# A two-layer hybrid trunk on one core: the norm's inverse root moved behind the input projections, the norm weight put on x ahead of them

## The chip, the cores and the metric

One core of a Trainium2 chip runs the whole kernel. The metric is device time in microseconds (us) of one launch. The kernel before takes 2810.47 us (median of 3 runs, 2808.8 to 2810.52).

## The reference, cut to what matters

256 tokens of width 4096 go through two layers. Each layer starts with an RMS norm and one wide input projection (w_in), whose columns feed four branches (S5, latent attention "MLA", gated linear attention "GLA", RG-LRU). The four results are gated and go through one output projection (w_out), which is added to x. A last RMS norm ends the trunk.

```python
def rms_norm(x, g):
    y = x * rsqrt(mean(x * x, axis=-1) + 1e-6)   # one inverse root r per token
    return y * g                                 # one weight g per column of x
# per layer:
h = rms_norm(x, norm_g)
z = h @ w_in      # = r * ((x * g) @ w_in): r belongs to the token, g to the summed index
# ... four branches on the columns of z, concatenated to y ...
x = x + y @ w_out
# at the end: out = rms_norm(x, final_g)
```

The latents of MLA (cq, ckv) are RMS-normalised again before they are used, and the gate columns of z go through SiLU.

## The kernel before

**Tiling.** Activations lie transposed: 128 partitions are 128 columns of x, 256 tokens lie along the free axis, and x is 32 such tiles (`zb`). Every large product is computed to float32 accuracy from two halves. An operand v is split into hi = v rounded to float32r and lo = v - hi. A chunk is 2 tiles of the summed index by 256 output columns, 256 KB of weights. For a chunk TensorE runs 4 matmuls of 512 columns (hi with hi and lo together) and 4 of 256 columns (lo with hi), lines 322, 323 and 325 in `chunk`. A layer has 914 chunks. 32 of them make a pair: two halves of 16 chunks, one for each half of the four accumulator banks.

**Stages of a layer.** Nine pairs of input projection, in which the S5 work of DVE and GpSimd goes on beside them ("pre" pairs); a middle stage (GLA values, S5's GLU, heads of MLA); eight gate pairs, one for each 128 columns of the branches; and eight pairs of output projection. The hb tiles hold the split activations.

**Order.** Every engine has its own instruction stream, written out by hand, in which a step number c (the chunk) says where small work goes. At step c ScalarE (ACT) copies the hi half of the weights of chunk c+3 (`hi`, line 626), once chunk c-1 is done, because `w2` has 4 buffers; VectorE (DVE) subtracts to get the lo half (`lo`, line 1049); TensorE runs chunk c. So DVE may be some three chunks late before TensorE stands. The sync engine (SP) loads weights into 8 raw buffers, each as soon as its old content is used. Finished accumulators are taken out by ACT (`evac`, line 632) and added by DVE (line 1055).

**The norm before.** In the prologue, ACT squares x as its eight parts of 512 KB land (line 649), DVE sums them (line 1181), GpSimd adds the sums (line 1638). TensorE turns the sums into one column per 128 tokens (`columns`, line 333, 12 matmuls), ACT takes the square root (line 637), DVE the reciprocal (line 1060), TensorE spreads it over the partitions (`spread`, line 342). Only then does DVE multiply x by g and r in one operation per tile (`h_mul`, line 1068), ACT rounds it (`split_hi`, line 642) and GpSimd subtracts (`split_lo`, line 1648); chunks 0 to 15 of a layer each wait for their pair of tiles. The same sequence stands between the two layers, behind the last evacuation. At the end, DVE multiplies the 32 tiles by r and final_g (line 1618), and four stores of 1 MB write them. The angles of the rotary embedding are also computed in the prologue (lines 1166 to 1173).

Of the kernel before, what the change touches and what calls it, by code (L numbers as in the profile page):

```python
# [18 lines left out]
P = 128  # L19
L = 2  # L20
# [50 lines left out]
PART_AT = {c + n: (p, kind, i, n, chunks) for p, (kind, i, c, chunks) in enumerate(PARTS) for n in range(chunks)}  # L71
Y_LAST = {5: 0, 8: 1, 11: 2, 16: 3, 21: 4, 22: 5}
# [22 lines left out]
def trunk(nc, w, x, pos, const, small, pg_in, s5raw, mixw_d, s5w_d, wg2_d, out):  # L95
# [3 lines left out]
    with ctx:  # L99
# [67 lines left out]
        rcol = sb("rcol", [P, 12])  # L167
        s5_all = sb("s5_all", [P, L, 3, 32])
# [26 lines left out]
        squares_made, sx_ready, x_ready = sem("squares_made"), sem("sx_ready"), sem("x_ready")  # L195
# [29 lines left out]
        x_added, x_saved = sem("x_added"), sem("x_saved")  # L225
# [39 lines left out]
        def _(sp):  # L265
            sp.dma_start(posi[:, :], pos.partition_broadcast(P)).then_inc(pos_loaded, 16)
            sp.dma_start(sm_all[:, :, :], small).then_inc(sm_loaded, 16)
            for i in range(8):
                sp.dma_start(zb[:, 4 * i:4 * i + 4, :], x[:, 4 * i:4 * i + 4, :]).then_inc(x_loaded[i], 16)
            sp.dma_start(kc[:, :], const).then_inc(const_loaded, 16)  # L270
            for s in range(RAW):
                sp.dma_start(raw[:, s], w[s]).then_inc(raw_loaded[s], 16)
# [26 lines left out]
            sp.wait_ge(x_stored, 16 * (1 + 16 * L))  # L299
# [3 lines left out]
        def _(pe):  # L303
# [83 lines left out]
            pe.wait_ge(const_loaded, 16)  # L387
            pe.wait_ge(consts_made, 1)

            for l in range(L):  # L390
                n_l, h_l, c_l = l * N_LAYER, l * H_LAYER, l * C_LAYER

                pe.wait_ge(sx_ready, l + 1)
                pe.wait_ge(last_squared, l + 1)
                columns([(sx, ssq[:, 0, :], ssq[:, 1, :])], B_Y)
                spread([ps[:, B_BU, 0:T]], c_l + 1)

                for c in range(CH_PAIR):
                    if c % CH_HALF == 0:
                        pe.wait_ge(acc_read, h_l + c // CH_HALF + 1)  # L400
# [19 lines left out]
                def k_turn():  # L420
                    pe.wait_ge(acc_read, h_l + H_MID + 2)
# [187 lines left out]
            pe.wait_ge(sx_ready, L + 1)  # L609
            pe.wait_ge(last_squared, L + 1)  # L610
# [5 lines left out]
        def _(act):  # L616
# [4 lines left out]
            def hi(n0, c, count=1):  # L621
# [4 lines left out]
                A(w2[:, d, :, 0, :], raw[:, s, :, :], ACT.Copy).then_inc(hi_ready, count)  # L626

# [17 lines left out]
            for i in range(8):  # L645
                act.wait_ge(x_loaded[i], 16)
                if i >= 2:
                    act.wait_ge(x_ready, i - 1)
                A(sqx[:, 4 * (i % 2):4 * (i % 2) + 4, :], zb[:, 4 * i:4 * i + 4, :], ACT.Square).then_inc(squares_made, 1)
                if i == 1:  # L650

                    act.wait_ge(consts_made, 1)
                    act.wait_ge(rope_made, 1)
                    A(gb[0:64, :], ga[0:64, :], ACT.Abs).then_inc(act_prep, 1)
                    act.wait_ge(act_prep, 1)
                    A(rope[0:64, :], gb[0:64, :], ACT.Sin, bias=HALF_PI[0:64], scale=-1.0).then_inc(act_prep, 1)
                    A(rope[64:96, :], ga[64:96, :], ACT.Sin, scale=-1.0).then_inc(act_prep, 1)
                    A(rope[96:128, :], ga[96:128, :], ACT.Sin).then_inc(act_prep, 1)

            for s in range(LOOK):  # L660
                act.wait_ge(raw_loaded[s], 16)
                act.wait_ge(chunk_done, s + 1)
                A(w2[:, s, :, 0, :], raw[:, s, :, :], ACT.Copy).then_inc(hi_ready, 1)

# [17 lines left out]
            def s5_inputs(it, g):  # L682

                act.wait_ge(bu_ready, it + 1)
                A(us[:, :], zb[:, g + Z_S5, :], ACT.Copy).then_inc(us_ready, 1)
# [7 lines left out]
            def s5_steps(it, g, more=True):  # L693
# [3 lines left out]
                if more:  # L697
                    steps[25] = [lambda: s5_inputs(it + 1, g + 1)]
# [3 lines left out]
            for l in range(L):  # L702
                n_l, h_l, c_l = l * N_LAYER, l * H_LAYER, l * C_LAYER
                rms(c_l + 1, 2, D, EPS1)
                split_hi(0, l * 32 + 1)
                split_hi(1, l * 32 + 2)
# [26 lines left out]
                pre_pair(1, {0: [lam_exponent], 2: [turn_sines], 25: [lambda: s5_inputs(l * G8, 0)],  # L733
                             31: [lambda: s5_tables(l * G8, 0)]}, one=True)
                own.restart()
                pre_pair(2, s5_steps(l * G8, 0))
                own.restart()
                with act.Fori(3, 8) as i:
                    pre_pair(i, s5_steps(l * G8 + (i - 2), i - 2))
                    own.restart()  # L740
                pre_pair(8, s5_steps(l * G8 + 6, 6))
# [8 lines left out]
                def latent_root():  # L750
                    act.wait_ge(cols_ready, c_l + 2)
                    A(ncol[:, 0:2], ps[:, B_Y, 0:2], ACT.Sqrt, bias=EPS1, scale=1.0 / QR)
                    A(ncol[:, 2:4], ps[:, B_Y, 2:4], ACT.Sqrt, bias=EPS1, scale=1.0 / KVR).then_inc(rms_ready, 1)
# [57 lines left out]
                for c in range(MID_END):  # L811
# [7 lines left out]
                    if c % CH_HALF == CH_HALF - 1 and (c < MID_GLU or MID_V3 <= c < MID_QKV):  # L819
                        h = H_MID + (c // CH_HALF if c < MID_GLU else 7)  # L820
                        evac(h_l + h, h % 2, n_l + (N_MID + c + 1))
                own.restart()

                for u in (9, 10, 14):
# [10 lines left out]
                def gate_pair(g, last=False):  # L835
# [102 lines left out]
                    def first_silu():  # L938
                        act.wait_ge(acc_read, h0 + 3)
# [5 lines left out]
                    def second_silu():  # L945
                        act.wait_ge(acc_read, h0 + 4)
# [17 lines left out]
                    for c in range(CH_PAIR):  # L964
                        if c > 0:
# [11 lines left out]
                hi(n_l + N_GATE, 0)  # L977
# [11 lines left out]
                def out_store(i, h, more):  # L989

                    act.wait_ge(outx, l * 16 + (i * 2 + (h + 1)))
                    act.dma_start(xres[:, bass.ds(i * 4 + 2 * h, 2), :], zb[:, bass.ds(i * 4 + 2 * h, 2), :]).then_inc(x_stored, 16)
                    if more:
                        old_x(h, bass.ds(i * 4 + (4 + 2 * h), 2))

                for c in range(CH_PAIR):
# [946 lines left out]
```

## Time and profile before

| | before |
|---|---|
| median of 3 runs | 2810.47 us |
| the profiled execution's own time | 2810.84 us |
| its span, first to last instruction | 2809.1 us |
| TensorE (PE) matmul busy | 2743.7 us, 98% of the span |
| VectorE (DVE) | 2065.9 us, 74% |
| ScalarE (ACT) | 1593.1 us, 57% |
| GpSimd (POOL) | 782.0 us, 28% |
| mean granted TensorE clock | 0.994 |

Busy time is the time in which an engine has an instruction under way. What is left of the span beside TensorE's 2743.7 us is some 65 us, and the stretches of the profile say where it lies. "Idle before" names the engine and line that ended a wait.

### The profile page before, as it was taken

How to read it: one execution, taken by the hardware profiler on the slowest of the kernel's cores; microseconds unless marked ns; L12 is line 12 of the kernel's file. 1: busy time of each engine (PE TensorE's matmuls, PEld its weight loads, DVE VectorE, ACT ScalarE, POOL GpSimd, SP SyncE). 2: the span in 40 equal slices, each digit the busy share in tenths (PEclk: the TensorE clock that was granted, in tenths of full speed). 3: DMA queues.
4: the chain of work that ended last, by engine and by line, in shares of the span. 5: the costliest groups of instructions: out<-in, count | busy, mean ns of one | idle time of the engine just before them, and what ended most of it. 6: DMA issues, size and time to landing. Idle time of an engine off the chain costs nothing.

```text
span 2809.1 us, 54381 instructions
## 1 busy us (share of the span) xinstructions
PE 2743.7 (98%) x15960; PEld 2358.4 (84%) x15960; DVE 2065.9 (74%) x3372; ACT 1593.1 (57%) x2867; POOL 782.0 (28%) x823
## 2 busy tenths in 40 slices
PE   5999999999999999999999999999999999999997
PEld 4888888888888888888878888888888888888886
DVE  8899999766666676555588999997666666855555
ACT  5555555656656665444455555556666656644443
POOL 3255555400110132111134555552011111411111
PEclk9999999999999999999999999999999999999998
DMA  6765566585655547777647666666765565577765
GB/s 218 254 189 173 185 177 188 168 262 175 187 174 168 188 148 219 210 210 210 207 143 210 179 183 175 187 176 184 248 188 170 172 185 166 178 213 210 210 210 175
DMA packets 294180, 538.72 MB, mean 192 GB/s; under 512 B 32432, under 2 KB 43584, under 8 KB 293056
## 3 DMA queue, kind: packets, MB, share of 16 engines
q1 hardware_dynamic: 268736, 497.45, 58.9%
q10 hardware_dynamic: 25344, 39.99, 4.2%
q8 instruction: 56, 0.92, 0.1%
q14 instruction: 44, 0.36, 0.0%
HBM read 516.34 MB, written 25.17 MB: 193 GB/s over the span
## 4 chain that ended last, share of the span: by engine, by line
PE 86%; DVE 7%; issue 3%; ACT 2%; POOL 1%; DMA 0%; ACTq 0%; DVEq 0%; SPq 0%; POOLq 0%
PE ps L323 53%; PE ps L322 26%; DVE w L1049 3%; PE ps L325 1%; ACT w L626 1%; DVE yy L1118 1%; POOL lg L1672 1%; DVE g L1112 1%; PE ps L354 1%; PE ps L333 1%; PE ps L365 0%; DVE zb L1618 0%; PE ps L342 0%; PE ps L502 0%; PE ps L501 0%
## 5 line engine op out<-in xcount | busy, mean ns | idle before, releaser
L323 PE MATMUL ps<-hb,w 128*128 128x512 f32 x5824 | 2051.9, 396 | 6.1 <-issue 6.1
L1049 DVE TENSOR_TENSOR w<-raw,w 128x512 fp32r<-128x512 f32 x1828 | 1338.0, 741 | 643.0 <-ACT w L626 633.0
L626 ACT ACTIVATE w<-raw 128x512 fp32r<-128x512 f32 x1828 | 1133.3, 628 | 935.6 <-PE ps L323 917.0
L322 PE MATMUL ps<-hb,w 128*128 128x256 f32 x5690 | 1617.1, 284 | 8.3 <-DVE w L1049 6.8
L323 PEld LDWEIGHTS ps<-hb,w 128*128 128x128 f32 x5824 | 1091.3, 188 | 254.5 <-issue 6.6
L322 PEld LDWEIGHTS ps<-hb,w 128*128 128x128 f32 x5690 | 1074.9, 189 | 44.5 <-DVE w L1049 17.4
L323 PE MATMUL ps<-gl,w 128*128 128x512 f32 x800 | 283.3, 395 | 0.0
L1810 POOL TENSOR_TENSOR nf<-zb 128x256 f32 (+1 forms) x60 | 52.0, 867 | 537.1 <-DVE zb L1586 531.6
L322 PE MATMUL ps<-gl,w 128*128 128x256 f32 x680 | 190.2, 280 | 0.0
L323 PE MATMUL ps<-w,hb 128*128 128x512 f32 x512 | 180.6, 395 | 0.0
L323 PEld LDWEIGHTS ps<-gl,w 128*128 128x128 f32 x800 | 149.5, 188 | 30.1
L1652 POOL TENSOR_TENSOR sx<-yl 128x256 f32<-128x256 f32 x16 | 15.7, 984 | 473.5 <-DVE yl L1452 473.5
L322 PE MATMUL ps<-w,hb 128*128 128x256 f32 x496 | 141.6, 286 | 1.5 <-DVE w L1049 1.0
L322 PEld LDWEIGHTS ps<-gl,w 128*128 128x128 f32 x680 | 128.1, 188 | 2.5
L1661 POOL TENSOR_SCALAR sx<-kc,pgp 128x256 f32<-128x256 f32 x64 | 73.3, 1145 | 185.2 <-POOLq L252 107.4
L323 PEld LDWEIGHTS ps<-w,hb 128*128 128x128 f32 x512 | 95.8, 188 | 21.2
L632 ACT ACTIVATE half_lo<-ps 128x512 f32<-128x512 f32 (+1 forms) x144 | 84.2, 585 | 42.3 <-PE ps L323 42.3
L1118 DVE TENSOR_TENSOR yy<-g,tab 128x512 f32<-128x512 f32 x64 | 103.9, 1623 | 0.0
L322 PEld LDWEIGHTS ps<-w,hb 128*128 128x128 f32 x496 | 93.6, 189 | 7.3 <-DVE w L1049 6.2
L1112 DVE TENSOR_TENSOR_SCAN g<-pgd,yy 128x256 f32<-128x256 f32 x128 | 86.8, 717 | 0.0
L1663 POOL TENSOR_SCALAR nf<-nf 128x256 f32<-128x256 f32 x64 | 64.2, 1003 | 5.6
L1652 POOL TENSOR_TENSOR sx<-yg 128x256 f32<-128x256 f32 x16 | 10.6, 662 | 187.8 <-ACT yg L920 187.8
(311 smaller groups left out, 2410.0 us busy)
## 6 DMA issues: line engine op xcount, KB each, us to landing
raw<-in_w SPq DMA_DIRECT2D x1843, 256.0 KB, 2.8
hd<-heads ACTq DMA_DIRECT2D x16, 512.0 KB, 5.2
gate<-xres ACTq DMA_DIRECT2D x32, 256.0 KB, 4.3
xres<-zb ACTq DMA_DIRECT2D x32, 256.0 KB, 3.6
zb<-in_x SPq DMA_DIRECT2D x8, 512.0 KB, 7.3
xres<-in_x SPq DMA_DIRECT2D x4, 1024.0 KB, 6.4
s5w<-in_s5w ACTq DMA_DIRECT2D x16, 256.0 KB, 3.4
out<-zb SPq DMA_DIRECT2D x4, 1024.0 KB, 3.9
```

The lines of the kernel that those rows point to most:

```text
L322: mm(acc[:, T:], a_lo, m_hi, start=False, stop=False, skip_group_check=True)
L323: last = mm(acc, a_hi, m_both, start=(k == 0), stop=(k == nk - 1), skip_group_check=True)
L325: last = mm(acc[:, T:], a_lo, m_hi, start=False, stop=False, skip_group_check=True)
L333: last = mm(ps[:, bank, 2 * i + b:2 * i + b + 1], s[:, P * b:P * b + P], ones[:, :], start=(n == 0), stop=(n == len(tiles) - 1))
L626: A(w2[:, d, :, 0, :], raw[:, s, :, :], ACT.Copy).then_inc(hi_ready, count)
L632: A(half_lo[:, 0:tiles, :], ps[:, 2 * half:2 * half + tiles, 0:T], ACT.Copy).then_inc(lo_copied, 1)
L1049: V.tensor_tensor(w2[:, d, :, 1, :], raw[:, s, :, :], w2[:, d, :, 0, :].bitcast(F), ALU.subtract).then_inc(w2_ready, count)
L1112: V.tensor_tensor_scan(g2[:, a, :], pgd[:, j:j + 1].to_broadcast([P, T]), yy[:, a, :], 0.0, ALU.mult, ALU.add).then_inc(scanned, 1)
L1118: V.tensor_tensor(yy[:, :, :], g2[:, ::-1, :], tab[:, 1:3, :], ALU.mult).then_inc(tab_used, 1)
L1661: own.do(G.tensor_scalar(sx[:, :], iota, f0, None, ALU.mult))
L1663: own.chain(G.tensor_scalar(nf[:, :], nf[:, :], -MAGIC, None, ALU.add))
L1810: own.chain(G.tensor_tensor(nf[:, :], z, z, ALU.mult))
```

## The change

Layer 0: x is multiplied by g alone as it arrives (DVE, one operation of two tiles), split by ACT and GpSimd, and the chunks start. The squares are summed by TensorE between chunks (`x_sums`, eight times 8 matmuls of one column). Root, reciprocal and spread come in steps 17 to 21 of the first pair; the rotary angles move to steps 19 and 23. Layer 1: ACT multiplies each new pair of x tiles by the next g during the output stage (`x_gain`), in the last output pair ACT and GpSimd split 15 of the 16 pairs of tiles, and the first pair of layer 1 only handles the last one; root in steps 6 to 10. The inverse root is kept as a spread tile `rs` and as a column `rch`, and is multiplied to results: `scale` (13 a layer) and `gates_scale` (16 a layer) are new DVE operations of 128x512 (one of the 13 is 128x256); the GLA values take it inside their evacuation (4 a layer, ACT and DVE each in two operations of 128x256); MLA's latents take it inside their own root. At the end ACT has put final_g on 30 tiles before, and DVE multiplies two tiles at a time by r. Two of the weight loads are issued behind each of the first four parts of x. In the gate stage a second chunk's hi and lo come ahead of the waits at each pair's border.

```diff
@@ SP
             for i in range(8):
                 sp.dma_start(zb[:, 4 * i:4 * i + 4, :], x[:, 4 * i:4 * i + 4, :]).then_inc(x_loaded[i], 16)
+                for s in range(2 * i, min(2 * i + 2, RAW)):
+                    sp.dma_start(raw[:, s], w[s]).then_inc(raw_loaded[s], 16)
             sp.dma_start(kc[:, :], const).then_inc(const_loaded, 16)
-            for s in range(RAW):
-                sp.dma_start(raw[:, s], w[s]).then_inc(raw_loaded[s], 16)
@@ PE
+            def x_sums(i):
+                pe.wait_ge(squares_made, i + 1)
+                pe.wait_ge(consts_made, 1)
+                for b in range(2):
+                    for q in range(4):
+                        last = mm(ps[:, (B_Y, B_A)[b], 0:1], sqx[:, 4 * (i % 2) + q, P * b:P * b + P], ones[:, :], ...)
+                last.then_inc(squares_used if i < 7 else cols_ready, 1)
-                pe.wait_ge(sx_ready, l + 1)
-                pe.wait_ge(last_squared, l + 1)
-                columns([(sx, ssq[:, 0, :], ssq[:, 1, :])], B_Y)
-                spread([ps[:, B_BU, 0:T]], c_l + 1)
                 for c in range(CH_PAIR):
...
                     chunk(n_l, c, c // CH_HALF)
+                    if l == 0 and c in X_SUMS:              # 2, 4, ... 16
+                        x_sums(X_SUMS.index(c))
+                    if l > 0 and c == ROOT_AT[l] - 1:       # ROOT_AT = (17, 6)
+                        pe.wait_ge(sx_ready, l)
+                        pe.wait_ge(last_squared, l)
+                        columns([(sx, ssq[:, 0, :], ssq[:, 1, :])], B_Y)
+                    if c == ROOT_AT[l] + 2:
+                        pe.wait_ge(const_loaded, 16)
+                        spread([ps[:, B_BU, 0:T]], c_l + 1)
@@ ACT
                 for c in range(CH_PAIR):
                     hi(n_l, c)
-                    if c + 2 < CH_HALF:
-                        split_hi(c + 2, l * 32 + (c + 3))
+                    if l == 0 and c + 2 < CH_HALF:
+                        split_hi(c + 2, c + 3)
+                    if l == 0 and c in (1, 3, 5, 7, 9, 11, 13):
+                        x_square((c + 1) // 2)
+                    if l == 0 and c == 23:
+                        rope_sines()
+                    if l > 0 and c == 0:
+                        last_x(l - 1)                       # waits for the last sum, squares it, stores it
+                    if l > 0 and c == 2:
+                        split_hi(15, l * 32 + 16)
+                    if c == ROOT_AT[l]: ...                 # the root
@@ ACT, middle to gate stage
+                hi(n_l + N_GATE, 0)
+                hi(n_l + N_GATE, 1)
                 for u in (9, 10, 14):
                     act.wait_ge(part_stored[u % 3], ...)
...
                 nc.scalar.preload_act_table_set("silu_and_others")
-                hi(n_l + N_GATE, 0)
+                act.wait_ge(scaled, l * 13 + 13)
@@ ACT, gate pair (DVE's has the same order)
                     def second_silu():
-                        act.wait_ge(acc_read, h0 + 4)
+                        act.wait_ge(gates_scaled, l * 16 + (g * 2 + 2))
...
                     if not last:
                         second_gates()
                         hi(n0, CH_PAIR)
+                        hi(n0, CH_PAIR + 1)
                         second_silu()
@@ ACT, output stage
+                def x_gain(i, h):
+                    act.wait_ge(x_squared, l * 15 + (i * 2 + (h + 1)))
+                    if l < L - 1:
+                        act.wait_ge(x_stored, 16 * (16 * l + 1) + (i * 32 + 16 * (h + 1)))
+                    for q in range(2):                      # z = one tile of x, gain = its column of g
+                        last = A(z, z, ACT.Identity, scale=gain)
+                    last.then_inc(x_gained, 1)
+                def split_x(p):                             # steps 4, 7, 10, 13, 21 to 31 of the last pair
+                    ...
+                    A(hb[:, 2 * p:2 * p + 2, 0, :], zb[:, 2 * p:2 * p + 2, :], ACT.Copy).then_inc(h_hi_ready, 1)
@@ DVE
+            def h_mul(p, l):
+                ...
+                V.tensor_tensor(hf[p % 3][:, :, :], zb[:, 2 * p:2 * p + 2, :], g, ALU.mult)
+            def scale(z, half):
+                dve.wait_ge(acc_read, half + 3)
+                V.tensor_tensor(z, z, spread_rs(z.shape[1]), ALU.mult).then_inc(scaled, 1)
...
                 for c in range(CH_PAIR):
                     lo(n_l, c)
-                    if c + 3 < CH_HALF:
-                        h_mul(c + 3, l * 32)
+                    if l == 0 and c + 3 < CH_HALF:
+                        h_mul(c + 3, l)
+                    if l > 0 and c == 1:
+                        h_mul(15, l)
+                    if c == ROOT_AT[l] + 1:
+                        layer_root()
+                    if c == ROOT_AT[l] + 4:
+                        layer_rs()
+                    if l == 0 and c == 19:
+                        rope_angles()
+                    if c == 22:
+                        scale(zb[:, 0:2, :], h_l)
+                    # unchanged: preparation of S5 at steps 16, 18, 20, ... 30
...
+                    def gates_scale(h):
+                        dve.wait_ge(acc_read, h0 + (h + 3))
+                        V.tensor_tensor(gate[:, h, :, :], gate[:, h, :, :], spread_rs(2), ALU.mult)
@@ DVE, the end
-            for k in range(KT):
-                last = V.scalar_tensor_tensor(out=zb[:, k, :], ..., in1=ps[:, B_BU, 0:T], ...)
+            for k in range(0, KT - 2, 2):
+                last = V.tensor_tensor(zb[:, k:k + 2, :], zb[:, k:k + 2, :],
+                                       ps[:, B_BU:B_BU + 1, 0:T].to_broadcast([P, 2, T]), ALU.mult)
@@ POOL
-            for i in range(1, 6):
-                G.tensor_tensor(sx[:, :], sx[:, :], ...)    # sums of the squares of x
+                def x_lo(p):                                # pairs 0 to 3, then 4 to 14, in the last output pair
+                    pool.wait_ge(h_hi_ready, (l + 1) * 32 + (p + 1))
+                    G.tensor_tensor(hb[:, 2 * p:2 * p + 2, 1, :], zb[:, 2 * p:2 * p + 2, :], ..., ALU.subtract)
```

## Rows read from the trace of the kernel before

**Rows 1.** Stretches of the span: for each engine busy us (instructions), then granted clock, DMA.

```profile
0.00:59.70 59.70, 31.58 (x145) 24.94 (x146) 47.94 (x69) 34.30 (x51) 25.82 (x31) 1.00 0.65 212
59.70:1402.30 1342.60, 1337.78 (x7829) 1152.22 (x7827) 987.76 (x1608) 768.52 (x1389) 365.65 (x388) 1.00 0.64 195
1402.30:1441.30 39.00, 32.05 (x145) 25.40 (x146) 29.75 (x53) 20.16 (x35) 21.53 (x16) 0.82 0.37 114
1441.30:2784.80 1343.50, 1338.37 (x7829) 1152.30 (x7827) 986.29 (x1608) 768.66 (x1390) 368.99 (x388) 1.00 0.63 190
2784.80:2809.10 24.30, 3.91 (x16) 3.56 (x16) 14.20 (x36) 1.48 (x3) 0.00 (x0) 0.55 0.45 184
```

**Rows 2.** Chain of waits, first 60 us: start, us, what.

```profile
24.05 2.70 PE ps L333 x12
...
41.51 0.78 DVE yy L1068 x2
42.30 0.92 DVE w L1049
```

**Rows 3.** Timeline of the first 62 us: start, us, instruction, [idle before].

```profile
6.23 1.06 ACT L649 ACTIVATE vb<-zb 128x1024 f32<-128x1024 f32 x1 [4.20 <-DMA zb<-in_x]
...
30.25 1.27 POOL L1648 TENSOR_TENSOR hb<-xx,hb 128x512 fp32r<-128x512 f32 x1 [9.27 <-ACT hb L642]
```

**Rows 4.** TensorE's timeline, first chunks of the two halves of pair 0.

```profile
59.80 0.28 PE L325 MATMUL ps<-hb,w 128*128 128x256 f32 x1
...
81.99 0.28 PE L325 MATMUL ps<-hb,w 128*128 128x256 f32 x1
```

**Rows 5.** Chain of waits between the layers.

```profile
1402.32 0.61 ACT half_lo L632
...
1409.70 3.03 issue
```

**Rows 6.** TensorE's timeline, middle stage: columns between two chunks.

```profile
522.39 0.95 PE L333 MATMUL ps<-ones,ssq 128*128 128x1 f32 x8
523.20 0.36 PE L322 MATMUL ps<-w,hb 128*128 128x256 f32 x1
```

**Rows 7.** VectorE's timeline: rotary angles to the first sum; second half of pair 0.

```profile
4.34 0.29 DVE L1166 CAST gab<-kext 128x256 f32<-128x256 int32 x1 [4.34 <-DMA sm_all<-in_small]
...
7.42 1.96 DVE L1181 TENSOR_REDUCE sx<-vb 128x256 f32<-128x1024 f32 x1
...
66.37 1.29 DVE L1049 TENSOR_TENSOR w<-raw,w 128x512 fp32r<-128x512 f32 x2
...
82.59 0.69 DVE L1055 TENSOR_TENSOR zb<-half_lo,ps 128x512 f32<-128x512 f32 x1 [0.25 <-ACT half_lo L632]
```

**Rows 8.** VectorE's timeline, middle stage, GpSimd busy beside it.

```profile
502.84 3.99 DVE L1049 TENSOR_TENSOR w<-raw,w 128x512 fp32r<-128x512 f32 x4
```

**Rows 9.** Timelines of ScalarE and VectorE at the border of two gate pairs.

```profile
779.82 0.60 ACT L632 ACTIVATE half_lo<-ps 128x512 f32<-128x512 f32 x1 [0.78 <-PE ps L323]
...
783.68 1.47 DVE L1049 TENSOR_TENSOR w<-raw,w 128x512 fp32r<-128x512 f32 x2 [0.84 <-ACT w L626]
...
785.98 0.69 DVE L1049 TENSOR_TENSOR w<-raw,w 128x512 fp32r<-128x512 f32 x1
```

**Rows 10.** Timeline from the middle to the gate stage.

```profile
626.81 1.28 ACT L976 ACT_TABLE_LOAD   x1 [1.42 <-ACTq L252]
...
629.51 0.38 PE L322 MATMUL ps<-hb,w 128*128 128x256 f32 x1 [1.05 <-DVE w L1049]
```

**Rows 11.** Timeline of the end; then the page's part on DMA issues.

```profile
2792.15 12.62 DVE L1618 SCALAR_TENSOR_TENSOR zb<-zb,sm,ps 128x256 f32<-128x256 f32 x32 [1.31 <-PE ps L342]
2795.40 9.74 SPq L296 DMA_DIRECT2D out<-zb  x4
...
zb<-in_x SPq DMA_DIRECT2D x8, 512.0 KB, 7.3
...
out<-zb SPq DMA_DIRECT2D x4, 1024.0 KB, 3.9
```

More of the change, by code:

```diff
@@ L626, in hi, with tokens_evac @@
                 A(w2[:, d, :, 0, :], raw[:, s, :, :], ACT.Copy).then_inc(hi_ready, count)
+            def tokens_evac(h0, half, n_done):
+                act.wait_ge(chunk_done, n_done + W2)
+                act.wait_ge(acc_read, h0 + 2)
+                for j in range(2):
+                    last = A(half_lo[:, j, :], ps[:, 2 * half + j, 0:T], ACT.Identity, scale=rch[:, j:j + 1])
+                last.then_inc(lo_copied, 1)
             def evac(h0, half, n_done, tiles=2):
@@ L697, in s5_steps @@
                 if more:
-                    steps[25] = [lambda: s5_inputs(it + 1, g + 1)]
+                    steps[25] = [lambda: s5_inputs(it + 1, g + 1, ready)]
                     steps[31] = [lambda: s5_tables(it + 1, 0)]
@@ L751, in latent_root @@
                     act.wait_ge(cols_ready, c_l + 2)
-                    A(ncol[:, 0:2], ps[:, B_Y, 0:2], ACT.Sqrt, bias=EPS1, scale=1.0 / QR)
-                    A(ncol[:, 2:4], ps[:, B_Y, 2:4], ACT.Sqrt, bias=EPS1, scale=1.0 / KVR).then_inc(rms_ready, 1)
+                    for i in range(4):
+                        last = A(ncol[:, i:i + 1], ps[:, B_Y, i:i + 1], ACT.Sqrt, bias=EPS1, scale=rvar[:, i:i + 1])
+                    last.then_inc(rms_ready, 1)
                 def glu_evac(m):
@@ L1139, in s5_skip, with s5_steps @@
                 own.do(V.tensor_copy(pgd[:, 4:5], pgl[:, g, C_S5D:C_S5D + 1]))
-            def s5_steps(it, g, first=False, more=True):
+            def s5_steps(it, g, ready=None, first=False, more=True):
                 steps = {}
@@ L1147, in s5_steps @@
                 steps[3] = [lambda: s5_scalars(g)] + steps[3]
-                steps[6] = ([] if first else [lambda: s5_tail(it - 1, g - 1)]) + [lambda: s5_skip(g)]
+                steps[6] = ([] if first else [lambda: s5_tail(it - 1, g - 1, ready)]) + [lambda: s5_skip(g)]
                 return steps
@@ L1331, in _, with pre_pair @@
                         evac(h_l + h, h, zb[:, 2 * h:2 * h + 2, :])
+                scale(zb[:, 2:4, :], h_l + 1)
                 own.restart()
[L1334 removed]
+                def pre_pair(i, steps, dst=None, scales=()):
                     for c in range(CH_PAIR):
@@ L1407, in _ @@
                 steps[73] = steps.get(73, []) + [lambda: reciprocals(c_l + 3, 2)]
+                for n in range(8):
+                    at = MID_QKV + 5 * n + 1
+                    z = zb[:, Z_QK + 2 * n:Z_QK + 2 * n + 2, :]
+                    steps[at] = steps.get(at, []) + [lambda n=n, z=z: scale(z, h_l + (6 + n))]
                 for c in range(MID_END):
@@ L1610, in _ @@
                             out_end(i, 0)
+                with dve.Fori(1, 8) as i:
+                    out_pair(i)
                 out_end(7, 1)
@@ L1714, in _ @@
                 h_l, c_l = l * H_LAYER, l * C_LAYER
-                for k in range(KT // 2):
+                for k in range(KT // 2) if l == 0 else (15,):
                     split_lo(k, l * 32 + (k + 1))
+                pool.wait_ge(const_loaded, 16)
                 pool.wait_ge(dve_prep, l + 1)
@@ L1816, in _ @@
                     own.restart()
+                if l < L - 1:
+                    for p in range(4):
+                        x_lo(p)
                 out_squares(7, 0)
@@ L1819, in _ @@
                 pool.sem_inc(sx_ready, 1)
+                if l < L - 1:
+                    for p in range(4, 15):
+                        x_lo(p)
 def _constants():
```

233 lines of the change are left out of this document (145 added, 88 removed).

## The prediction

> **What bounds the kernel now.** I read the stretches first, then the chain of waits, then the timelines. The stretches [rows 1] show two kinds of time. In 59.7 to 1402.3 and in 1441.3 to 2784.8 us TensorE (PE) has a matmul under way for 1337.8 of 1342.6 and 1338.4 of 1343.5 us: it is the bound, and it stands for 10 us in all. The other three stretches are different: the first 59.7 us hold 145 PE instructions, the 39.0 us between the layers hold 145, the last 24.3 us hold 16. Sixteen chunks at full pace would need little: pair 0's chunk 16 starts at 59.80 and chunk 32 at 81.99 [rows 4], so a chunk is 22.19 / 16 = 1.39 us and sixteen are 22.2. In the first stretch PE waits 24 us for the sum of squares, then goes at the pace of DVE, which needs 0.78 us for h_mul and 0.92 for lo, 1.70 per chunk [rows 2]. Between the layers the same chain runs again from 1402.32 until a last gap of 3.03 us before the first chunk [rows 5], and the clock is granted at 0.82 on the mean there [rows 1], the low level of 1.2 GHz after PE had stood. So there are three places to win, and all else must stay under a PE that is always busy.
>
> **Start, layer 0.** The first part of x can be read at 6.23 us [rows 3]; then come DVE's multiply (0.7), ACT's split (0.60, by the 128x512 of [rows 9]) and GpSimd's subtraction (1.27 [rows 3]), which with handovers is 9.1 us for chunk 0. Pace after that, for each chunk. PE: 1.39 plus half of a group of 8 columns; such a group pushed the next chunk back by 523.20 - 522.39 = 0.81 [rows 6], so 1.80. ACT: two copies of 0.60 and half a square of 1.06 [rows 3, 9], 1.73. DVE: two operations that read SBUF alone; one takes 0.60 undisturbed (two in 1.29, the first of them 0.60 [rows 7]) and 3.99 / 4 = 1.00 beside a busy GpSimd [rows 8]. In GpSimd's 1.27 DVE does 0.76 of its 1.20, the rest takes 0.44, so 1.71. Three engines within 0.1 us of each other do not run at the best of them: I take 1.85, 29.6 for sixteen. I add 2.4 for the filling (the first chunks pass through the three engines one behind the other, and PE starts at the low clock) and 1.4 for data: eight parts of x, each landing 7.3 us after its issue [rows 11], now share the engines with weights, and chunk 8 is loaded last of all. Chunk 16 starts at 9.1 + 29.6 + 2.4 + 1.4 = 42.5 in place of 59.80: **-17.3**. Ends: 1.80 a chunk with nothing added gives -21.9; 2.47 (below) gives -7.4.
>
> **Second half of pair 0, layer 0.** DVE has no idle time from before 66.37 until 0.25 us ahead of 82.59 [rows 7]; it is late already, under the cover of the three chunks that are prepared ahead. The change adds at steps 18 to 22: five small operations of the root (1.0), the rotary angles (4.34 to 7.42, 3.08 [rows 7]), the copy of rs (0.35) and a scale (0.60), 5.0 in all. The cover: step 19's lo ends at 66.97 and its chunk 22 starts at 59.80 + 6 x 1.39 = 68.1, 1.2 us; later steps have about 1.7. PE is itself put back by the last group of columns and the spread, 0.81 + 0.5. So PE stands 5.0 - 1.7 - 1.3 = 2.0, and 0.4 for the scale behind step 31: **+3.7** with the 1.3. If the cover were gone, +5.4 + 1.3; if DVE caught up, +1.3. ACT's two table loads there (1.28 each, [rows 10]) lie in that cover.
>
> **Between the layers.** Chunk 16 of layer 1 starts 39.0 us after layer 0's last chunk; with 15 pairs of tiles ready it is sixteen chunks, 22.2, plus what PE now does among them: 12 columns at 0.10 and a spread of 4 matmuls, 0.5. 39.0 - 22.2 - 1.7 gives **-15.1**. What covers the rest: in the last output pair ACT has two copies a chunk, 1.2 of 1.39 us, and GpSimd 1.27 of 1.39; both keep up, barely. x_gain waits for the store of its tiles, nine steps after its issue. `last_x` holds ACT at step 0 until DVE's second sum, about 2.1 us after the last chunk; behind it in ACT's queue are a square, a DMA issue and step 1's hi, and PE has three chunks, 4.2 us. Root operations at step 7 meet a DVE with half its time free. Ends: -5 (ACT late by a chunk or two, and PE at the low clock again) and -16.8.
>
> **Middle to gate stage.** PE stood 1.05 us for DVE, which stood for ACT, which waited 1.42 for stored parts and loaded a table (1.28) before its hi [rows 10]. Two hi's now go ahead: **-2.0** for two layers. Next late is step 2's hi, with two chunks of room.
>
> **Operations added under a busy PE.** 29 of DVE a layer. Most cost nothing while PE is the bound. Where DVE is the late one they count: 0.35 for kg before S5's first step, and 0.6 to 0.75 where the last gate pair meets the output stage (DVE multiplies y there each step), 0.15 for the values: 1.25 a layer, **+2.5**. Below nothing is excluded, since they only add.
>
> **Borders of gate pairs, 14 of them.** Queued behind the added wait on ACT (silu for gates_scale) is step 2's hi; PE waits for that. The last chunk ends at 779.8 [rows 9]. Before, DVE prepared chunks 4 and 5 in one go from 783.68, a full loop restart (0.84) after the gating. Now chunk 4 is ready by 783.0, ahead of the wait; then gates_scale, silu, gating and restart put chunk 5's lo at 784.95 to 785.55, and PE needs it at 779.8 + 5 x 1.39 = 786.75. 1.2 us are left, as before: 0. GpSimd's copies wait for the gating too, and land within that.
>
> **End.** 32 operations take 12.62, 0.394 each [rows 11]. Fifteen of two tiles with r in PSUM at 0.60 (as DVE's sum of [rows 7], start to start) and two old ones are 9.8, so 2.8 less. The last store begins behind the last of them and takes 3.9 [rows 11]; the four could now queue behind one another, so **-2.5**. Ends 0 and -2.8.
>
> Sum: -17.3 + 3.7 - 15.1 - 2.0 + 2.5 - 2.5 = -30.7. From the profiled execution's 2810.84 that is 2780.1; the median of the runs, 2810.47, is 0.4 below it, inside the rounding. **2780 us.**
>
> **Rivals.**
> 1. *DVE and GpSimd shut each other out at the start.* Then a chunk costs 2 x 0.60 + 1.27 = 2.47, sixteen 39.5, and the time is 2790. For it: DVE's 1.00 in place of 0.60 [rows 8]. Against it: before, lo beside GpSimd's subtraction would then need 0.60 + 1.27 = 1.87 a chunk, and the chunk took 1.70 [rows 2]. Chance 0.12. The Trainium skill (SBUF — State Buffer, on the shared port pair) states this as a rule: a DVE operation with both inputs in SBUF and a GpSimd operation that reads SBUF hold the pair in turn for the whole instruction, so h_mul, which leaves PSUM, would pay; by that rule the time is this rival's, and the trace bears the slowing out but not the full exclusion.
> 2. *The gate pairs' borders stall.* If the 1.2 us are gone and one more is missing, 14 borders cost 14 us: 2794. For it: ACT now waits twice for DVE in a pair. Against: PE stands nowhere in the gate pairs now, and 4.8 us in the whole stretch [rows 1]. 0.07.
> 3. *The last output pair's splits come late.* ACT has 1.2 of 1.39 us; with evacuations it falls behind, PE stands and falls to the low clock: 10 us less won, 2790. 0.05.
> 4. *More is won.* The start runs at 1.80 with no data wait and DVE's lag is absorbed: 4 + 2 us more, 2774. 0.12.
> 5. *Slower than before.* The price is each of the 58 added DVE operations on PE's path, because DVE is the late engine in S5 and gate stages: at 1.00 each (beside GpSimd [rows 8]) 58 us, less the 2.5 counted: 2836; at 0.60, 2812, no change. It decides from (30.7 + 2.5 + 5.6) / 58 = 0.67 us each. For it: DVE's 988 us in the long stretch are in part dense. Against: the S5 pairs proper get none of them, and DVE is at 74% there on the mean [rows 1]. 0.04, half of it slower.
>
> **How the numbers follow.** Forecast 0.60 (2774 to 2786 on its own); the rivals as given. From 2810.47, 0.2% (5.6 us, about what a measurement can tell from none) is 2804.9 and 2816.1. All but rival 5 are faster: 0.95 with rounding; same 0.02; slower 0.03. The range reaches to rivals 1, 3 and 4 and as far as rival 2: 2771 to 2794.
>
> **What would show it.** Chunk 0 at 9 us and chunk 16 at 42 to 43; a chunk every 1.85 us before; PE gaps of some 2 us in all between 45 and 70 us, with DVE busy throughout; no gap over 1 us and a clock of 1.00 between the layers, chunk 16 of layer 1 some 24 us after layer 0's last; no wait of 1.05 at the gate stage; DVE's last stretch 9.8. I would be wrong if PE gaps repeat at each gate pair, if GpSimd's subtractions and DVE's multiplies alternate strictly at the start, or if the start waits for weights by more than 2 us.

## The result: 2795.1 us, 0.55% less than before, and the profile after

The median of five runs is 2795.13 us (2791.7 to 2797.0) against 2810.47 before; the ratio is 0.9945, with a 95% interval of 0.993 to 0.996. The kernel is faster, but the forecast of 2780 is 15 us too low and the range ended 1.1 us short. The profiled execution took 2791.7 us (span 2789.9), 3.4 us less than the median, so 11.6 us of the miss can be read in the trace.

The stretches of the changed kernel, cut where [rows 1] were cut (columns as there):

```profile
0.00:48.60 48.60, 38.17 (x241) 34.02 (x242) 31.62 (x36) 28.29 (x44) 23.50 (x26) 1.00 0.78 273
48.60:1399.40 1350.80, 1341.84 (x7850) 1155.11 (x7849) 1018.82 (x1655) 793.60 (x1449) 387.39 (x401) 1.00 0.63 193
1399.40:1425.20 25.80, 24.77 (x146) 21.32 (x145) 17.65 (x28) 11.31 (x21) 5.33 (x4) 1.00 0.57 185
1425.20:2765.00 1339.80, 1334.99 (x7810) 1149.99 (x7809) 1008.02 (x1640) 779.65 (x1423) 365.93 (x388) 1.00 0.62 188
2765.00:2789.90 24.90, 6.47 (x36) 5.42 (x34) 13.45 (x23) 2.75 (x5) 0.00 (x0) 0.64 0.41 169
```

The first stretch went from 59.7 to 48.6 us and TensorE has work in 38.2 of them. Between the layers the granted clock is 1.00 (before 0.82). TensorE's first matmul is at 9.7 us. Its timeline, at the matmul by which chunks 0, 16 and 32 can be told (it answers to [rows 4]):

```profile
10.27 0.41 PE L332 MATMUL ps<-hb,w 128*128 128x256 f32 x1
...
48.63 0.28 PE L332 MATMUL ps<-hb,w 128*128 128x256 f32 x1
...
76.49 0.28 PE L332 MATMUL ps<-hb,w 128*128 128x256 f32 x1
```

Chunk 16 came 11.2 us earlier and not 17.3, and the half behind it took 27.9 us and not 25.9. The starts of all 144 halves in both traces (the "marks" below) divide the change of the span as follows (us, after minus before):

| Step | Forecast | Traces |
|---|---|---|
| start, to chunk 16 | -17.3 | -11.2 |
| second half of pair 0, layer 0 | +3.7 | +5.7 |
| between the layers | -15.1 | -13.4 |
| middle to gate stage, two layers | -2.0 | -2.2 |
| added VectorE operations elsewhere | +2.5 | +4.7 |
| borders of gate pairs | 0 | 0 |
| end | -2.5 | -2.8 |
| sum | -30.7 | -19.2 |

The row between the layers runs to chunk 32 of layer 1. To chunk 16, where the forecast for it ended, the traces give -13.0; the half behind it took 22.19 us for 22.60, a difference that halves of one kernel also show among themselves.

How the start runs now. TensorE's timeline at the third group of column sums, to be held against [rows 6]:

```profile
26.73 1.84 PE L401 MATMUL ps<-ones,vb 128*128 128x1 f32 x16
28.43 0.36 PE L329 MATMUL ps<-hb,w 128*128 128x256 f32 x1
```

The group puts the next chunk back by 28.43 - 26.73 = 1.70 us, twice the 0.81 that I took from [rows 6]. The cause is in the counts: a matmul of these float32 sums stands as two instructions in the trace, so the "x8" of [rows 6] were four matmuls, and the "x16" here are the eight of the code. (The chunks' matmuls, which take float32r, stand as one each. The 12 and 4 that I counted for the columns and the spread were instructions too, of six and two matmuls; their price, taken per instruction, was not hurt by it.) TensorE's period is thus some 2 x 1.46 + 1.70 = 4.62 us for two chunks (most groups start 4.59 to 4.61 apart), and behind its first matmul no single gap of over 0.3 us shows up to 48 us. In the same stretch the timeline of VectorE (DVE) and GpSimd (POOL) shows something else:

```profile
19.24 1.30 POOL L1788 TENSOR_TENSOR hb<-yy,hb 128x512 fp32r<-128x512 f32 x1 [0.39 <-ACT hb L669]
19.32 1.77 DVE L1150 TENSOR_TENSOR g<-zb,sm_all 128x512 f32<-128x512 f32 x1
...
21.62 0.68 DVE L1150 TENSOR_TENSOR xx<-zb,sm_all 128x512 f32<-128x512 f32 x1
21.84 1.59 POOL L1788 TENSOR_TENSOR hb<-g,hb 128x512 fp32r<-128x512 f32 x1 [1.29 <-ACT hb L669]
```

The multiply by the norm weight takes 0.68 us alone, and 1.77 when GpSimd's subtraction has begun 0.08 before it: it ends 0.55 behind the subtraction. The other way round the subtraction takes 1.59. This is the strict alternation that the prediction named as a sign against itself. So there were two explanations of the lost 6.1 us, TensorE's matmuls or the exclusion, and the experiments had to tell them apart.

### The profile page after: what moved, and what is told of

It is laid out like the page before. It is cut to its first block, busy times and chain, and to the rows that moved or that the text cites. A ratio compares the mean times of both kernels' runs of the same rounds, so it can differ in the third digit from the quotient of the medians.

```text
span 2789.9 us, 54823 instructions
## 1 busy us (share of the span) xinstructions
PE 2746.3 (98%) x16076; PEld 2365.9 (85%) x16076; DVE 2089.6 (75%) x3380; ACT 1615.6 (58%) x2940; POOL 782.1 (28%) x818
## 4 chain that ended last, share of the span: by engine, by line
PE 89%; DVE 5%; issue 2%; ACT 2%; POOL 1%; DMA 0%; ACTq 0%; DVEq 0%; SPq 0%; POOLq 0%
PE ps L330 54%; PE ps L329 27%; DVE w L1130 2%; PE ps L332 1%; ACT w L645 1%; PE ps L361 1%; PE ps L372 1%; PE ps L401 0%; PE ps L520 0%; PE ps L340 0%; PE ps L521 0%; POOL lg L1812 0%; PE ps L349 0%; PE ps L539 0%; DVE yy L1217 0%
## 5 line engine op out<-in xcount | busy, mean ns | idle before, releaser
L1952 POOL TENSOR_TENSOR nf<-zb 128x256 f32 (+1 forms) x30 | 26.7, 889 | 517.6 <-DVE zb L1722 517.6
L1136 DVE TENSOR_TENSOR zb<-half_lo,ps 128x512 f32 (+1 forms) x68 | 46.2, 679 | 20.3 <-ACT half_lo L659 20.3
```

The source lines that it names most:

```text
L1136: V.tensor_tensor(dst, half_lo[:, 0:tiles, :], ps[:, 2 * half:2 * half + tiles, T:], ALU.add).then_inc(acc_read, 1)
```

## The experiments

Each kernel was timed in five runs beside the kernel before, which stood at 2808.5, 2809.7 and 2808.9 us in the three groups of runs. The changed kernel itself spreads over 5 us, so I take a median of five as uncertain by about 1 us, and a difference between two groups carries up to 1.2 us more, by which the kernel before moved. Differences below are plain ones of two medians; where less matters I go by the marks.

**The changed kernel again.**

> The changed kernel as it is, a second time, for a profile and for its time beside the others of this group. Expected 2791 to 2797 us. The first five times of it were 2791.7 and 2792.5 (two) and 2795.1 to 2797.0 (three), more apart than those of the kernel before. If one place in the program sets it, a profile that falls among the upper times shows 3 to 5 us more in that place alone and the same marks elsewhere; if it is spread out, the marks drift apart all along.

2793.25 us (2791.13 to 2795.91). Marks against the first trace: chunk 16 at 48.94, chunk 32 at 76.74, the last half within 0.14 us. What moves between these two executions is mostly the S5 pairs. TensorE's waits in pairs 3 to 7 of layer 0 (180 to 300 us; engine, line, waited for: us in total, times, longest): the first trace has

```profile
PE ps L329 <- DVE w L1130: 0.9, 2, 0.6
```

and the second has none. Single pairs in 185 to 380 and 1530 to 1770 us are 0.5 to 0.75 longer in one execution than in another, of the same kernel or of another; the first half of the gate stage moved by 0.9 in one trace, too. The expectation spoke of a profile among the upper times, and this one fell on the lowest of its five, as the first had. So none of the upper times was profiled, and what they have more is open. In these two traces the differences lie in several pairs and not in one place.

**Fewer sums: is TensorE the bound at the start?** Six of the eight groups keep one matmul of eight (`if 0 < i < 7 and (b, q) != (1, 3): continue`); then, in another kernel, every group keeps half (`for q in range(2)`). Both leave out a part of the sum of squares.

> Of the eight groups of column sums of x's squares at the start, the six in the middle are cut from eight matmuls to one, so the root is taken of a part of the columns. Theory (TensorE sets the pace of the first half, and each group costs it 1.68 us, 0.21 a matmul): the period of two chunks falls from 4.6 towards 3.1 us, and chunk 16 starts 5.5 to 8.8 us earlier than in the changed kernel (8.8 = 6 x 7 x 0.21); the whole time falls by as much. Rival (VectorE and GpSimd delay each other while they split x, and TensorE has slack for the groups): the period stays over 4.0 us, chunk 16 comes 2 us earlier at most, and TensorE shows idle time where the sums were.

> Every group of column sums has four matmuls in place of eight (the other half of the squares is left out of the sum). Theory: 0.84 us less in each of eight groups, so 5.9 us less before chunk 16 and 0.8 behind it, 6.7 in all. Rival (another engine sets the pace): 2 us or less. Together with the run that cuts six groups to one matmul this gives the price of a matmul and the point at which another engine takes over.

2793.15 and 2791.84 us: 0.1 and 1.4 below the changed kernel. In the second of them chunk 16 started at 48.04. My theory falls. In the first, one of TensorE's groups from 0 to 62 us shows who was next:

```profile
L329 PE MATMUL ps<-hb,w 128*128 128x256 f32 x90 | 27.6, 306 | 9.6 <-POOL hb L1790 7.5 <-DVE w L1132 1.8 <-DVE w L1284 0.3
```

Matmuls worth 8.8 us (42 at 0.21) were taken away before chunk 16, which came at 47.68, 1.0 to 1.3 earlier, and TensorE now stands 7.5 us for GpSimd's x.

**The same with nothing left out: bfloat16 sums.**

```
- A(sqx[:, 4*(i%2):4*(i%2)+4, :], zb[...], ACT.Square)       # sqx float32, ones float32
+ A(sqx[:, 4*(i%2):4*(i%2)+4, 0:T], zb[...], ACT.Square)     # sqx, ones_b bfloat16
```

> ScalarE writes the squares of x as bfloat16 and the ones column is bfloat16, so that a column sum is one pass of TensorE and not two; nothing else differs. Theory (the two passes of 0.105 us each are what the start pays): each group falls from 1.68 to 0.84 us or less, 5.9 us less before chunk 16 and 6.7 or more in all. Rival (the pace is set by another engine, or the price of such a matmul is a fixed latency and not its passes): less than 2 us.

2791.08 us, 2.2 less and not 6.7; the theory failed here too. TensorE's timeline at the same group as above:

```profile
26.72 0.35 PE L402 MATMUL ps<-ones_b,vb 128*128 128x1 bf16 x8
28.08 0.39 PE L330 MATMUL ps<-hb,w 128*128 128x256 f32 x1 [1.01 <-POOL hb L1790]
```

The group fell from 1.70 to 0.35 us, more than I had expected, and the chunk behind it came 0.35 earlier: a wait of 1.01 took the place. Chunk 16 at 47.85, 0.8 to 1.1 earlier.

**Is it a ring of handovers or the exclusion?** By the exclusion, a VectorE operation with both inputs in SBUF and a subtraction of GpSimd, which reads SBUF too, run one after the other. The other theory was a ring of handovers between engines: I followed VectorE, ScalarE and GpSimd round in that trace and found a closed one of 4.58 us with ScalarE's square in it. Two edits, both on top of the bfloat16 sums, tell them apart.

```
- if l == 0 and c in (1, 3, 5, 7, 9, 11, 13): x_square((c + 1) // 2)
+ if l == 0 and c in (2, 4, 6, 8, 10, 12, 14): x_square(c // 2)
```

> The bfloat16 sums, and ScalarE's square of two chunks stands one chunk later, behind its split of an even chunk and no more behind that of an odd one. Theory: the ring of split, square 0.95, weight split 0.52, split 0.69, GpSimd 1.30, VectorE 0.55 and the odd split 0.54 again, 4.58 us for two chunks, loses the 0.95 of the square: 3.6 us, and chunk 16 comes at 41 to 42 us in place of 47.9; 6 us less in all than with the bfloat16 sums alone, 2785. Rival (the ring closes by another way, or data set the pace): chunk 16 within 2 us of 47.9.

```
+ own.chain(V.tensor_copy(ps[:, B_BU, 0:KT], sm_all[:, 0, S_NORM:S_NORM + KT]))     # once
- g = sm_all[:, l, S_NORM + 2*p:S_NORM + 2*p + 2]...
+ g = ps[:, B_BU, 2*p:2*p + 2]...                                                  # layer 0
```

> The bfloat16 sums, and the norm weight read from PSUM. Theory (VectorE with two inputs in SBUF and GpSimd exclude each other for a whole operation; the multiply leaves that with one input in PSUM): the multiplies fall from 1.77 to 0.68 us, the pace becomes that of TensorE (3.3 us for two chunks) or ScalarE (3.1), with VectorE's weight subtractions still excluded: 3.3 to 3.8, chunk 16 at 39 to 43 us, 5 to 8 us less in all than with the bfloat16 sums alone, 2783 to 2786. Rival (what delays the multiply is the queue of handovers and not the memory of its operand): multiplies stay at 1.77 and chunk 16 within 2 us of 47.9.

The square moved: 2791.23 us, chunk 16 at 47.99, nothing won. The norm weight in PSUM: 2787.57 us, chunk 16 at 43.03. That chunk came 4.8 us earlier, at the late end of what I expected; the time is 3.5 less and not 5 to 8. The square in the ring was not the bound. With the square moved, VectorE's groups from 15 to 38 us and then its timeline beside GpSimd's read:

```profile
L1131 DVE TENSOR_TENSOR w<-raw,w 128x512 fp32r<-128x512 f32 x11 | 13.6, 1237 | 0.1
```

```profile
21.73 0.68 DVE L1151 TENSOR_TENSOR xx<-zb,sm_all 128x512 f32<-128x512 f32 x1
21.95 1.58 POOL L1790 TENSOR_TENSOR hb<-g,hb 128x512 fp32r<-128x512 f32 x1 [1.29 <-ACT hb L670]
22.42 1.66 DVE L1131 TENSOR_TENSOR w<-raw,w 128x512 fp32r<-128x512 f32 x1
23.49 1.74 POOL L1790 TENSOR_TENSOR hb<-xx,hb 128x512 fp32r<-128x512 f32 x1
...
24.00 1.77 DVE L1151 TENSOR_TENSOR yy<-zb,sm_all 128x512 f32<-128x512 f32 x1
```

VectorE has no idle time left (0.1 us in 23). GpSimd's end at 23.53 and 25.23, VectorE's at 22.41, 24.08 and 25.77, so one of VectorE's comes 0.55 behind GpSimd's last and one of GpSimd's 1.12 to 1.15 behind VectorE's: the two take turns. Two chunks take 4.58 to 4.65 us. With four VectorE operations at 0.60, GpSimd's share is (4.65 - 2.40) / 2 = 1.12 us an operation. (Where the square keeps its place, as in the changed kernel, VectorE stands 0.96 us for ScalarE while a subtraction of GpSimd runs; moved, it is shut out in the same time.) With the weight in PSUM the groups of VectorE from 15 to 38 us are

```profile
L1153 DVE TENSOR_TENSOR g<-zb,ps 128x512 f32<-128x512 f32 x4 | 2.7, 678 | 0.0
L1153 DVE TENSOR_TENSOR yy<-zb,ps 128x512 f32<-128x512 f32 x4 | 2.7, 677 | 0.0
L1153 DVE TENSOR_TENSOR xx<-zb,ps 128x512 f32<-128x512 f32 x4 | 2.7, 676 | 0.0
```

every multiply at 0.68 beside the same subtractions, while VectorE's weight subtractions, both inputs in SBUF, still take 1.20 when they meet one. Five of the seven intervals between groups of sums are now 3.1 to 3.5 us in place of 4.6; the other two are 5.2, which was there before, and 5.5. The longer one comes behind a wait of ScalarE for weights, its cause most likely; of ScalarE's waits of 15 to 45 us:

```profile
ACT w L646 <- DMA raw<-in_w: 2.4, 1, 2.4
```

**The fourth corner.** The weight in PSUM with the float32 sums.

> VectorE's multiply of x by the norm weight reads the weight from a copy in PSUM (made once, one small operation), so that it has one input in SBUF and not two; the sums stay in float32. Theory (two limits lie on top of each other at the start, both 4.6 us for two chunks: TensorE with its float32 sums, and a ring of VectorE, ScalarE and GpSimd in which VectorE's multiply stands still until GpSimd's subtraction is over): with the ring alone broken TensorE still takes 4.6, chunk 16 stays within 1 us of 48.6 to 48.9, and VectorE's multiplies of 1.77 us become 0.68. Rival (VectorE and GpSimd alone set the pace): chunk 16 comes 5 us earlier or more.

2792.13 us, chunk 16 at 48.51. The multiplies are short here too, and nothing is won, as expected; the groups of sums start 4.57 apart. VectorE's groups from 16 to 36 us (two of them):

```profile
L1130 DVE TENSOR_TENSOR w<-raw,w 128x512 fp32r<-128x512 f32 x11 | 10.2, 930 | 6.1 <-ACT w L645 6.0
L1152 DVE TENSOR_TENSOR xx<-zb,ps 128x512 f32<-128x512 f32 x4 | 2.7, 676 | 0.0
```

VectorE, freed, stands 6 us. The four kernels together settle the start (first matmul of chunk 16, us):

| | weight in SBUF | weight in PSUM |
|---|---|---|
| float32 sums (4.6 us of TensorE for two chunks) | 48.63, 48.94 | 48.51 |
| bfloat16 sums (2 x 1.39 + 0.35 = 3.1 us) | 47.85 | 43.03 |

Two limits of 4.6 us lay on each other; either edit alone is worth 0.1 to 1.1 us, both together 5.6 to 5.9. Three more kernels below have the start of the changed one, with chunk 16 at 48.45 to 49.23, so the single gains are near what this mark varies by, and the joint one is far above it.

**Second half of pair 0.** The rotary tables go to pair 1.

```
- if l == 0 and c == 19: rope_angles()      # VectorE
+ # pair 1, step 9: rope_angles()
- if l == 0 and c == 23: rope_sines()       # ScalarE
+ # pair 1, step 11: rope_sines()
```

> The rotary angles (VectorE) go from step 19 of pair 0 of layer 0 to step 9 of pair 1, and their sines (ScalarE) from step 23 to step 11 of pair 1; nothing is left out. Theory: they stand ahead of the root and the weight splits in the second half of pair 0, where TensorE is idle for 2.0 and 0.5 us, and there is slack in pair 1: 2 to 3 us less. Rival (those gaps are the root's own chain of PE, ScalarE and VectorE): the gaps stay, 0.5 us or less; if pair 1 has no slack for them, no change in the sum, and the gap shows in pair 1.

2791.91 us. The gaps of the changed kernel, in TensorE's timeline, and the angles in VectorE's, are

```profile
62.30 0.39 PE L329 MATMUL ps<-hb,w 128*128 128x256 f32 x1 [1.76 <-DVE w L1130]
64.20 0.39 PE L329 MATMUL ps<-hb,w 128*128 128x256 f32 x1 [0.24 <-DVE w L1130]
67.76 0.39 PE L329 MATMUL ps<-hb,w 128*128 128x256 f32 x1 [0.51 <-DVE w L1130]
```

```profile
57.88 0.69 DVE L1130 TENSOR_TENSOR w<-raw,w 128x512 fp32r<-128x512 f32 x1
...
59.85 1.34 DVE L1274 SCALAR_TENSOR_TENSOR gab<-gab 128x256 f32<-128x256 f32 x3
...
61.56 0.69 DVE L1130 TENSOR_TENSOR w<-raw,w 128x512 fp32r<-128x512 f32 x1
```

Two weight splits are 3.68 us apart because of them. Moved, the gaps are gone and the half takes 24.7 us in place of 27.8, 3.1 less; but pair 1 gives back 1.5 (marks against the second trace of the changed kernel: -2.9 behind pair 0, -1.4 at pair 2). The time is 1.3 less: the cost was rightly placed, and the cover in pair 1 is half of what I took.

**The scalings in the heads stage.**

```
- at = MID_QKV + 5 * n + 1
+ at = (45, 46, 49, 50, 51, 76, 77, 78)[n]
```

> VectorE's eight scalings of the q, k and recurrence inputs of each layer move from the stage of the heads to steps of the middle stage (steps 45, 46, 49 to 51 and 76 to 78). Theory: they cost the heads stage 1.2 us in layer 0 and 0.9 in layer 1, where VectorE is what TensorE waits for; moved, 2.1 us less in all. Rival (the loss there is the later start of what follows, not the scalings): no change within 0.5 us; or the middle stage pays for them: slower.

2792.70 us, 0.6 less. The marks say more than the time. The heads stage with its mixing took 52.37 us in the changed kernel and 51.12 here in layer 0, 52.0 and 51.1 in layer 1: 1.25 + 0.9 won there, as expected, and both are back at the 51.12 of the kernel before. The same trace is 1.3 longer in the S5 pairs of layer 0, by waits of the kind shown above, which vary without an edit. The groups of VectorE from 568 to 624 us, first in the changed kernel and then here:

```profile
L1159 DVE TENSOR_TENSOR zb<-zb,rs 128x512 f32<-128x512 f32 x8 | 5.5, 684 | 0.0
```

```profile
L1159 DVE TENSOR_TENSOR zb<-zb,rs 128x512 f32<-128x512 f32 x2 | 1.4, 686 | 0.0
```

Six fewer stand in the stage, and no single wait of TensorE was over 0.4: by the marks the loss lies in four steps of the stage, 0.2, 0.2, 0.6 and 0.3 us.

**The order at the gate stage.** `hi(n_l + N_GATE, 0)` and `hi(n_l + N_GATE, 1)` go back behind the wait for the stored parts and the table load.

> ScalarE's first two weight splits of the gate stage are put back behind the wait for the stored parts and the change of its function table, as in the kernel before, in both layers. Theory (this order is what gave 1.3 and 0.9 us at the start of the gate stage): 2.0 to 2.2 us slower than the changed kernel, in those two places. Rival (the gain there came from less work ahead of it on VectorE): within 0.5 us.

2795.79 us, 2.5 more. The half in front of the gate stage is 26.83 and 26.74 us in place of 25.5 and 25.65, 1.3 + 1.1, and the wait of [rows 10] is back in TensorE's timeline:

```profile
626.91 0.39 PE L329 MATMUL ps<-hb,w 128*128 128x256 f32 x1 [1.06 <-DVE w L1130]
```

In the changed kernel ScalarE's timeline has the two splits ahead of the load:

```profile
623.61 0.63 ACT L645 ACTIVATE w<-raw 128x512 fp32r<-128x512 f32 x1 [0.94 <-ACTq L259]
...
624.15 0.62 ACT L645 ACTIVATE w<-raw 128x512 fp32r<-128x512 f32 x1
624.78 1.28 ACT L1024 ACT_TABLE_LOAD   x1
```

**All together**, first without the two edits of the ring, then with them.

> The bfloat16 column sums, the later rotary tables and the moved scalings together. Theory, if the three shortfalls are separate: the sum of the three single gains, 6.7 + 2.5 + 2.1 = 11.3 us less than the changed kernel, 2784 us beside a median of 2795. Rival (they share a cover, so that the time comes back at the next wait): 7 us less or under.

> Everything that should help, in one kernel: bfloat16 sums, norm weight in PSUM, the square one chunk later, the rotary tables in pair 1, the scalings of the heads in the middle stage. Theory: the 2787.6 us without the two changes of the ring, less 7 to 9: 2779 to 2781 us. Rival (VectorE, which stands behind in the second half of pair 0, gives back what the first half wins): 2784 or more.

2787.62 and 2785.83 us. The first is 5.6 us below the changed kernel run again and not 11.3; alone the sums brought 2.2, the tables 1.3 and the scalings 0.6, 4.1 in all. The second is the best kernel of this study, 7.4 us below it and 0.9919 of before (0.9906 to 0.9933). Both missed their expectations, and the rivals held. In the second, chunk 16 came at 43.75, but of the 9.1 us that it led by behind pair 0 it had 6.9 at pair 2 and 6.1 at the end: pair 1, with the rotary tables in it, is 2.1 us longer. In the kernel with the weight in PSUM and the tables left where they were, the lead stayed (6.8 behind pair 0, 6.7 at pair 2, 5.7 at the end). The best one also shows ScalarE waiting 2.8 us for weights once in the start, and one interval of 7.6 us there between groups of sums, where the others are 3.1 to 3.6. Which of these a further edit would free was not tried.

## Why the prediction was wrong, point by point

**Start, -17.3 for -11.2.** This is the step that failed: the pace of a chunk, forecast 1.85 us and measured 2.3, mis-sized in two terms. *"PE: 1.39 plus half of a group of 8 columns; such a group pushed the next chunk back by 0.81"*: the row was four matmuls shown as eight instructions; a group costs 1.70, and TensorE's pace is 2.3 a chunk and not 1.80. *"In GpSimd's 1.27 DVE does 0.76 of its 1.20, the rest takes 0.44, so 1.71"*: VectorE does nothing of it while GpSimd's operation has its turn; the pace is 2 x 0.60 + 1.12 = 2.32. Either term alone would have been enough to hold the start where it was. The 1.00 of [rows 8] was a mean over operations that met GpSimd (three of 1.10 to 1.23 us) and one that did not (0.68), and I read it as a slowing of all. Nearly right was chunk 0 (forecast 9.1, it was 9.7). The allowance of 3.8 for filling and data, too, was more than was needed: 38.4 us from the one mark to the other are 16 x 2.32 and 1.3.

**Rival 1 was half of the mechanism, with too small a chance.** It gave 2790, and the profiled execution took 2791.7. That closeness is luck: its start of -7.4 is 3.8 short of the measured one, and the other steps together lost 5.4 more than the sum had; and it says nothing of TensorE's sums, which alone hold the same pace. My argument against it was that with full exclusion the kernel before would need 0.60 + 1.27 = 1.87 a chunk, and took 1.70 [rows 2]. But 1.27 is an operation from start to end; what it excludes is 1.12, and 0.60 + 1.12 = 1.72 is what the kernel before took to 0.02 us. Its timeline has the turns in it, and I had not looked:

```profile
42.22 0.99 DVE L1049 TENSOR_TENSOR w<-raw,w 128x512 fp32r<-128x512 f32 x1
...
43.04 1.33 POOL L1648 TENSOR_TENSOR hb<-yy,hb 128x512 fp32r<-128x512 f32 x1 [0.38 <-ACT hb L642]
...
43.92 1.00 DVE L1049 TENSOR_TENSOR w<-raw,w 128x512 fp32r<-128x512 f32 x1
```

They end at 43.21, 44.37 and 44.92, so GpSimd's comes 1.16 behind VectorE's and VectorE's 0.55 behind GpSimd's, 1.71 together. The trace of before bore the rule out, and I read it as against it. The Trainium skill (SBUF — State Buffer, "SBUF: two separate sides") states just this: a VectorE operation with two inputs in SBUF and a GpSimd operation that reads SBUF get the shared port pair one after the other, each for its whole length. The runs agree: 1.77 us with both inputs in SBUF, 0.68 with one in PSUM, beside the same GpSimd operation. Had I gone by it with the 1.12, chunk 16 would have been at 9.1 + 37.1 + 3.8 = 50.0 us, the start -9.8 and the sum -23.2.

**Second half of pair 0, +3.7 for +5.7.** Right in place and kind (gaps of 2.0 and 0.5 us with VectorE late). The last group of columns was 0.9 too cheap for the reason above; the rotary angles stood in one block of 3.1 us ahead of a weight split, and moving them gave 3.1 of the 5.6 back. The bfloat16 sums gave another 0.9 there.

**Between the layers, -15.1 for -13.4 (-13.0 to chunk 16).** Idle time and clock came as forecast, but for one gap. In the last output pair GpSimd's and VectorE's operations meet; groups of 1378 to 1402 us, then VectorE's timeline at the end of the pair and the gap in TensorE's:

```profile
L1130 DVE TENSOR_TENSOR w<-raw,w 128x512 fp32r<-128x512 f32 x16 | 20.9, 1340 | 3.2 <-ACT w L645 3.1
...
L1960 POOL TENSOR_TENSOR hb<-zb,hb 128x512 fp32r<-128x512 f32 x11 | 18.2, 1689 | 1.4 <-ACT hb L1104 1.3
```

```profile
1395.42 6.88 DVE L1130 TENSOR_TENSOR w<-raw,w 128x512 fp32r<-128x512 f32 x4
```

```profile
1404.98 0.36 PE L329 MATMUL ps<-hb,w 128*128 128x256 f32 x1 [0.89 <-DVE w L1130]
```

*"GpSimd 1.27 of 1.39; both keep up, barely"* failed: a subtraction of GpSimd takes 1.69 there, and the last four of VectorE 6.88, 1.72 each; 0.60 + 1.12 is 1.72 and not under 1.39. The two chunks up to the end of that gap took 1.4 us more than two at full pace (1402.45 - 1400.75 and 1404.98 - 1402.45, for 1.39 each), and the last half of the output stage 22.44 for 22.19, which makes 1.7. That this is what is missing (1.7, or 2.1 to chunk 16) fits, but no run took the exclusion away in this place; it stays argued.

**Middle to gate, -2.0 for -2.2**, right, and shown by undoing it (+2.4). **Borders of gate pairs, 0**: right, all 14 are as long as before; rival 2 is refuted. **Added operations, +2.5 for +4.7**: the last gate pairs gave 1.5, near the 1.3 in the sum; missed were the scalings in the heads stage, 2.1 in all, which I had put under a busy TensorE. They are shown by moving them. The remaining 1.1 lies in front of the heads stage, most of it in the S5 pairs, about what those vary by; no run placed it.

**End, -2.5 for -2.8**, right; VectorE's last stretch, forecast 9.8, is 9.05 + 0.86, answering to [rows 11]:

```profile
2774.95 9.05 DVE L1760 TENSOR_TENSOR zb<-zb,ps 128x512 f32<-128x512 f32 x15 [1.32 <-PE ps L349]
2783.93 0.86 DVE L1765 SCALAR_TENSOR_TENSOR zb<-zb,sm,ps 128x256 f32<-128x256 f32 x2
```

**The median.** The other 3.4 us are the profiled execution against the median of its five. Run again the kernel had 2793.25, inside the range; ten runs lie between 2791.1 and 2797.0.

## What to carry to other kernels

Before taking a duration from a row, make sure what its count counts: hold it against the code, since one matmul of the float32 sums is two instructions here. When a mean lies between "undisturbed" and "excluded", look at the single operations before calling it a slowing, and test an exclusion against the period of the loop with start-to-start times, not with whole durations. And where one limit is removed, work out the second one before you promise its time: at this start two limits of 4.6 us hid each other, so that experiments on either alone showed 1.1 us at most, and only the pair of edits told them apart.

## What the runs showed of the hardware

- VectorE's multiply of 128x512 with both inputs in SBUF takes 0.68 us alone and 1.77 when a GpSimd subtraction began just before it; with one input in PSUM it takes 0.68 in both cases. GpSimd's takes 1.27 to 1.30 alone and, beside VectorE, up to 1.75 in one trace of the start and 1.83 in another. In strict alternation an operation of VectorE accounts for 0.60 and one of GpSimd for 1.12.
- Eight matmuls of 128 rows against one column cost TensorE 1.70 us in float32 (16 instructions) and 0.35 in bfloat16 (8 instructions), a factor of 4.9, where I had expected two.
- Executions of one and the same kernel differ by up to 5.9 us (2791.1 to 2797.0). The two that were profiled, each the shortest of its five (2791.7 and 2791.1), differ in single S5 pairs by 0.5 to 0.75 us either way; where the longer ones lose their time, and why, was not found.
